# Moving the building of the diagonal tap weights in a two-layer decoder kernel

## The reference

```
def swiglu(x, w_gu, w_down):
    a, b = jnp.split(x @ w_gu, 2, axis=-1)
    return (jax.nn.silu(a) * b) @ w_down
...
for i in range(DEPTH):
    x = layer_norm(ALPHA * x + 0.5 * swiglu(x, ffn1_w_gu[i], ffn1_w_down[i]), ...)
    # layer 0: gated linear attention; layer 1: a causal depthwise convolution, 31 taps per channel
    ...
    x = layer_norm(ALPHA * x + concat([y, m]) @ w_out, ...)
    x = layer_norm(ALPHA * x + 0.5 * swiglu(x, ffn2_w_gu[i], ffn2_w_down[i]), ...)
```

## Time and profile before

| | us |
|---|---|
| three timed runs | 2041.99, 2045.09, 2046.26 |
| median | 2045.09 |
| span of the profiled execution | 2042.9 |
| TensorE busy | 2022.1 |
| VectorE busy | 1354.6 |
| ScalarE busy | 810.9 |
| GpSimd busy | 806.1 |

### The profile page before, as it was taken

One profiled execution on the slowest core, in us unless ns is written; L12 is line 12 of the kernel. 1 busy time (PEld: TensorE's weight loads), 2 busy tenths in 40 slices (PEclk: granted clock), 3 DMA queues, 4 the chain that ended last, 5 costly groups with the idle time before them and its releaser, 6 DMA issues.

```text
span 2042.9 us, 34356 instructions
## 1 busy us (share of the span) xinstructions
PE 2022.1 (99%) x13509; PEld 1855.9 (91%) x13509; DVE 1354.6 (66%) x1843; ACT 810.9 (40%) x1165; POOL 806.1 (39%) x513
## 2 busy tenths in 40 slices
PE   9999999999999999999999999999999999999998
PEld 9899998988988999999899999889887799999887
DVE  4477774553434768787456878646899886776645
ACT  5433352263423354444234444423453434434422
POOL 1588830033323348871015888001100435887000
PEclk9999999999999999999999999999999999999999
DMA  7533333332201234443232545233544322332232
GB/s 251 207 123 123 123 129 104 99 105 83 63 31 62 93 114 155 154 155 109 93 107 93 165 146 170 97 96 107 178 126 172 103 74 92 103 103 92 91 102 87
DMA packets 229514, 239.14 MB, mean 117 GB/s; under 512 B 5999, under 2 KB 222189, under 8 KB 227628
## 3 DMA queue, kind: packets, MB, share of 16 engines
q1 hardware_dynamic: 228780, 235.68, 35.3%
q10 hardware_dynamic: 640, 2.16, 0.3%
HBM read 215.80 MB, written 22.02 MB: 116 GB/s over the span
## 4 chain that ended last, share of the span: by engine, by line
PE 91%; POOL 3%; DVE 2%; ACT 2%; issue 1%; DMA 1%; DVEq 0%; SPq 0%; ACTq 0%; POOLq 0%
PE bank L1835 12%; PE bank L1837 12%; PE bank L1836 12%; PE bank L1964 11%; PE bank L1966 11%; PE bank L1965 11%; PE bank L1846 4%; PE bank L1847 4%; PE bank L1848 4%; PE bank L1918 1%; POOL wlo L532 1%; ACT whi L711 1%; PE bank L1923 1%; PE bank L2271 1%; PE bank L2270 1%
## 5 line engine op out<-in xcount | busy, mean ns | idle before, releaser
L711 ACT CAST whi<-raw 128x2048 fp32r<-128x2048 f32 (+3 forms) x190 | 322.1, 1696 | 868.0 <-POOL scratch L593 434.2
L1173 DVE TENSOR_TENSOR wlo<-raw,whi 128x2048 fp32r<-128x2048 f32 (+2 forms) x164 | 354.7, 2163 | 234.4 <-ACT whi L711 233.9
L570 POOL TENSOR_TENSOR tiny<-tiny 128x2 f32<-128x2 f32 (+1 forms) x13 | 9.4, 725 | 572.0 <-DVE tiny L1448 572.0
L589 POOL TENSOR_TENSOR raw<-raw 128x512 f32<-128x512 f32 x72 | 221.5, 3076 | 0.0
L1835 PE MATMUL bank<-h_hi,whi 128*128 128x512 f32 x528 | 207.1, 392 | 0.0
L1836 PE MATMUL bank<-h_lo,whi 128*128 128x512 f32 x528 | 205.5, 389 | 0.0
L1837 PE MATMUL bank<-h_hi,wlo 128*128 128x512 f32 x528 | 205.5, 389 | 0.0
L593 POOL TENSOR_TENSOR scratch<-raw,s 128x512 f32<-128x512 f32 x72 | 152.8, 2123 | 48.7 <-DVE ex_lo L1180 48.7
L1964 PE MATMUL bank<-t_hi,whi 128*128 128x256 f32 x576 | 163.7, 284 | 1.6 <-DVE bank L1240 1.6
L1964 PE MATMUL bank<-t_hi,ex_hi 128*128 128x256 f32 x576 | 163.7, 284 | 1.0 <-DVE bank L1232 0.5
L1965 PE MATMUL bank<-xlo,whi 128*128 128x256 f32 x576 | 163.0, 283 | 0.0
(11 more groups left out here) (363 smaller groups left out, 5938.2 us busy)
## 6 DMA issues: line engine op xcount, KB each, us to landing
raw<-in_ffn_w_gu_dram SPq DMA_DIRECT2D x88, 1024.0 KB, 4.9
raw<-in_ffn_w_down_dram SPq DMA_DIRECT2D x32, 896.0 KB, 5.0
raw<-in_ffn_w_down_dram SPq DMA_DIRECT2D x32, 512.0 KB, 3.4
raw<-in_gla_w_in_dram SPq DMA_DIRECT2D x14, 1024.0 KB, 5.1
early_raw<-in_conv_w_in_dram SPq DMA_DIRECT2D x18, 512.0 KB, 4.2
lo_scratch<-early_lo SPq DMA_DIRECT2D x18, 512.0 KB, 3.3
diag_scratch<-diag_tmp SPq DMA_DIRECT2D x8, 1024.0 KB, 7.6
raw<-in_conv_w_in_dram SPq DMA_DIRECT2D x16, 512.0 KB, 5.5
```

What stands on the lines that cost most here:

```text
L589: nc.gpsimd.tensor_tensor(a21, a21, a11, ALU.add).then_inc(w_sum, 1)
L711: nc.scalar.copy(whi[:, s, 0:kc, 0:width], raw[:, s, 0:kc, 0:width]).then_inc(hi_ready, 1)
L1173: nc.vector.tensor_tensor(wlo[:, s, 0:kc, 0:width], raw[:, s, 0:kc, 0:width], whi[:, s, 0:kc, 0:width].bitcast(F32), ALU.subtract).then_in ...
```

## The change

Batches 0 to 2 stay. Batches 3 and 4 are built after the last sums of the first block, where 6 and 7 stood, and no batch stands between the seven products. Batches 5, 6 and 7 are built by GpSimd in the second block after the norm that precedes it and ahead of its weight sums, and SyncE stores them between the loads of the second block's first chunks. A store now moves only the taps that a batch has (7 of 8 for batches 4 to 7). VectorE's wait in the first block is for five stores instead of eight, and SyncE waits for all eight before it loads early_raw in the second block.

```diff
--- before.py
+++ after.py
@@ -79,7 +79,7 @@
 GLU_EVAC = [2, 4, 6, 8, 14, 16, 18, 20]
 LATE = 3
 TAPS_K = [8, 8, 7, 7]
-DIAG_PAIR = [3, 5, 7]
+DIAG_DOWN = [3, 4]
 PE_TAPS = sum(TAPS_K)
 
 
@@ -347,7 +347,8 @@
 
                 def diagonal_store(d):
                     sp.wait_ge(diag_built, d + 1)
-                    sp.dma_start(diag_dram[d // 2, d % 2], diag_tmp[:, :, :].bitcast(F32)).then_inc(diag_stored, 16)
+                    kc = TAPS_K[d // 2]
+                    sp.dma_start(diag_dram[d // 2, d % 2, :, 0:kc, :], diag_tmp[:, 0:kc, :].bitcast(F32)).then_inc(diag_stored, 16)
 
                 if f == 0:
                     for i in range(FK // 2):
@@ -357,8 +358,6 @@
                         load(n0 + 2 * i + 1, 1, cols(w_gu, i * 256 + FF))
                         if i == 1:
                             diagonal_store(1)
-                        if i - 1 in DIAG_PAIR:
-                            diagonal_store(3 + DIAG_PAIR.index(i - 1))
                 else:
                     def gate_and_up(i):
                         load(n0 + 2 * i, 0, cols(w_gu, i * 256))
@@ -373,9 +372,20 @@
 
                     w_conv = a["conv_w_in"][0].rearrange("(k p) n -> p k n", p=P)
                     if f < 3:
+                        d = DIAG_DOWN[-1] + 1
                         gate_and_up(0)
-                        gate_and_up(1)
-                        gate_and_up(2)
+                        if f == 1:
+                            load(n0 + 2, 0, cols(w_gu, 256))
+                            diagonal_store(d)
+                            load(n0 + 3, 1, cols(w_gu, 256 + FF))
+                            diagonal_store(d + 1)
+                            load(n0 + 4, 0, cols(w_gu, 512))
+                            diagonal_store(d + 2)
+                            load(n0 + 5, 1, cols(w_gu, 512 + FF))
+                            sp.wait_ge(diag_stored, 16 * 2 * len(TAPS_K))
+                        else:
+                            gate_and_up(1)
+                            gate_and_up(2)
                         sp.wait_ge(x_ready, x_base((LN_GLA_OUT, LN_FFN[1])[f - 1]) + DK)
                         early_load(0)
                         with sp.Fori(3, FK // 2) as i:
@@ -398,10 +408,10 @@
                     sp.wait_ge(early_done, EARLY * f + 1)
                     early_store(EARLY - 1)
                 if f == 0:
-                    diagonal_store(6)
+                    diagonal_store(DIAG_DOWN[0])
                 down_loads(0, (2, 3))
                 if f == 0:
-                    diagonal_store(7)
+                    diagonal_store(DIAG_DOWN[1])
                 with sp.Fori(1, 4) as p:
                     down_loads(p, range(4))
 
@@ -627,9 +637,7 @@
             for i in range(PLAIN, FK // 2):
                 weight_sums(0, i, 0)
                 weight_sums(0, i, 1)
-                if i in DIAG_PAIR:
-                    diagonal(3 + DIAG_PAIR.index(i))
-            for d in (6, 7):
+            for d in DIAG_DOWN:
                 diagonal(d)
             norm(LN_FFN[0])
 
@@ -659,6 +667,8 @@
             spare_lo_parts(LN_GLA_OUT, GLA_OUT_N)
             split_lo_blocks(GLA_OUT_N + 7, 1, B_K, after_dve=True)
             norm(LN_GLA_OUT)
+            for d in range(DIAG_DOWN[-1] + 1, 2 * len(TAPS_K)):
+                diagonal(d)
             all_weight_sums(1)
             norm(LN_FFN[1])
             all_weight_sums(2)
@@ -1406,7 +1416,7 @@
                             for d in range(4, DK):
                                 scaled_x(ln, d)
                         if f == 0 and p == 0:
-                            dve.wait_ge(diag_stored, 16 * 2 * len(TAPS_K))
+                            dve.wait_ge(diag_stored, 16 * (DIAG_DOWN[-1] + 1))
                         residual_pair(ln, p, n0 + 4 * p + 4, 0.5, DOWN_BANKS[p], (n0 + 4 * p + 5, 1, DOWN_K[1]),
                                       (4, 5) if p == 2 else ())
 
```

## The result

The changed kernel took 2052.02 us (median of 6 runs, 2050.26 to 2055.74) against 2044.63 us for the kernel before on the same chip (6 runs, 2041.77 to 2046.26): ratio 1.0035, 95% interval 1.0026 to 1.0045. It is slower by 0.35%, which is over the 0.2% that can be told from no change. The forecast was 2052.0. The profiled run is the shortest of the six, 2050.26 us, with a span of 2048.5 against 2042.9.

A forecast was written before the change was run, and what follows sets the result against it. TensorE, busy for 2022.1 of 2042.9 us, was taken as the bound. Terms -2.6 + 9.0 + 0.6 + 0.1 = +7.1 us on the median of 2045.09 gave 2052; 8-in-10 range 2043.5 to 2057.5.

The forecast's parts named there:

- The gain: First block: moving three builds and stores from between the products saves 2.6 us, bounds nothing and 3.79.
- The three waits: First block: TensorE's product waits for VectorE after builds between the products, starts 142.63, 176.62 and 225.28; these go.
- I take nothing: First block's down products: the now eight-tap build, 3.76 us for 3.33, adds at most 0.43 us, counted as nothing.
- the fourth wait: First block's last pair, at 286.90: TensorE's product waits 1.05 us for h_lo beside a build; it stays.
- The relay: Second block: one tile forces build, store, landing, build, store, landing, build, from 733.5 to 757.
- The rival in which the relay fits: Second block: landings under about 4.8 us let the builds fit; time 2042 to 2048, chance 0.23.
- The port: Second block: builds and VectorE's two-input instructions exclude each other; without this the sum would be some 2 us smaller.
- The late loads: Second block: loads queued behind stores wait for builds; fourth load goes at 738, ScalarE's cast moves from 739.89 to 746.
- The first sum: Second block: GpSimd's first weight sum starts at 757.9 instead of 749.06, 8.8 us late.
- Its slack: Second block: TensorE's second product has 1.06 us of slack behind the extra low parts, making the delay 7.8 us.
- the sums of the second chunk: Second block: they take the port twice instead of once before the extra parts; 1.3 us at most, 1.2 taken.
- The clock: Second block: TensorE's granted clock falls from 2.4 to 1.2 GHz after the waits; 0 to 1.5 us, 0.6 taken.

The follow-up runs named there:

- e1: Changed kernel with batches 5 to 7 neither built nor stored, stored batch 4 read instead: 2044.07 us, ratio 0.9997 to the kernel before.
- e4: Changed kernel, complete, with each store of the second block issued one load later: 2049.32 us, ratio 1.0019 to the kernel before.
- e8: Changed kernel with zero fills for the last three builds and each of their stores one load later: 2045.73 us, ratio 1.0006 to the kernel before.
- e3: Changed kernel with zero fills of the same length for the last three builds; stores, waits and queue kept: 2047.93 us, ratio 1.0017 to the kernel before.
- e5: Kernel before, complete, with batch 7 alone built later, after the fourth low part of the first block's down products: 2042.97 us, ratio 0.9987.
- e2: Changed kernel with batches 5 to 7 built back to back, not stored, loads in the old order: 2049.51 us, ratio 1.0029 to the kernel before.
- e6: Complete; batch 3 after pair 3, 4 after the last sums, 5 to 7 in three blocks' down products: 2041.36 us, ratio 0.9987 to the kernel before.
- e7: Complete; only batch 7 built in the second block, 5 and 6 in the first block's down products: 2048.96 us, ratio 1.0025 to the kernel before.
- e9: e7 with its one second-block store issued one load later: 2046.31 us, ratio 1.0002 to the kernel before.

## Why the prediction was right, step by step

The time, 2052.02 against 2052.0, is nearer than the steps are.

**The gain, forecast 2.6.** Six profiles have this first block (the changed kernel, e1 to e4 and e8). Their matmuls are 2.1 to 2.7 us ahead at the end of the products and 1.9 to 2.7 ahead after the last pair; in the changed kernel it is 2.49 and 1.92. The three waits went as said. "I take nothing" for the eight-tap build in the down products doesn't always hold, since the fourth wait grew in four of the six (1.46, 1.3, 1.4 and 1.1 us; 0.9 in e3 and e8):

```profile
284.99 0.39 PE L1974 MATMUL bank<-t_hi,whi 128*128 128x256 f32 x1 [1.46 <-DVE bank L1250]
```

1.46 us idle against 0.89 in the earlier trace rows. The weight split ahead of it on VectorE, beside the build, took 2.31 us at 279.58; before, the same one took 1.74, and 1.22 in e5 without a build beside it. The build began 0.46 us ahead of the split, where before it was 1.03; the eight-tap build in front of it is 0.43 us longer. e5 shows this wait to be the build's, since it goes with it.

**The relay, forecast 23.5 us long, ending 757.** Measured 4.32 + 5.03 + 3.84 + 4.84 + 4.54 = 22.6 us. The builds cost more than the 3.9 taken and the landings less than the 5.6. The rival in which the relay fits needed landings of less than about 4.8 us with builds of 3.4. e8 comes to that, with landings of 4.04 and 4.82 and a relay of 18.9 us: it cost 3.2 us in the second block, where the first block had gained 2.7, and its time can't be told from that of the kernel before. So the relay by itself doesn't make the kernel slower; it takes the builds' reads, or the late loads, on top.

**The port, an addition of "some 2 us".** The sizes were right. The prediction let the x sums beside the first build end the third chunk's split 2.6 us late (738.38 to 741); it was 2.7 (4.87 us behind the norm's end before, 7.55 after). It gave t_lo 3 us beside the third build (755 to 758), and it was 2.99. It gave each build about a microsecond, and the three took 0.99, 0.51 and 1.21 more. (The "1.4 us more" that it read for the h_lo pair is 1.5, 2.77 against 1.29 in e5.) What it had wrong is the weight: "without it the sum below would be some 2 us smaller". Without the reads (e3) the cost is 3.8 us smaller, and with the builds alone (e2), no store and no late load, it is 7.3. The relay was put first, and by itself it cost less than half of what the builds did. In the changed kernel the three ends tie, which hid this from the forecast of the time.

**The late loads.** Forecast: fourth load at 738, cast at 746 instead of 739.89, 6.1 later. The cast came 743.22 - 731.38 = 11.84 us after the norm's end, 6.38 before: 5.5 later. That "all three releases come at about the same time" is what was measured, relay at 753.91 and t_lo at 754.99, the first sum at 755.33. The raw weights came earlier than the 755 forecast: the second late load landed at 744.93 + 7.08 = 752.01.

**The first sum, forecast 8.8 us late:** 24.0 - 15.6 = 8.4. **Its slack, 1.06, and the sums of the second chunk, 1.2 at most:** from the first sum to the end of the extra low parts it is 768.88 - 755.33 = 13.55 us against 12.75, so 0.8. That gives 8.4 - 1.06 + 0.8 = 8.1, and TensorE's second product started at 768.93, 8.2 us late: 6.06 later than in the earlier trace rows, where the norm's end came 2.13 later.

**The clock, forecast 0.6:** from the second product on the matmuls fell another 1.6 us behind (6.06 to 7.65). The fall was twice as long as those of the kernel before, and what of it lay outside the waits was underrated. The cost of the block comes out at 9.6 to 9.8 where 9.7 was said: the first sum and the second chunk 0.8 too dear, the clock and the pairs behind 0.9 too cheap. That these cancel is luck.

**The rest of the kernel, forecast nothing:** -2.0 us in this profile (7.65 behind to 5.66). 1.5 of it is a clock fall near 1650 us that this execution doesn't have, 1.2 are waits of before that it doesn't have later in the second block, and 0.7 is lost in the third. No step of the change is there, and e1, without the three batches, differs from the kernel before in the same way at 1650 and in the third block, so I take it for chance; the other five runs are 0.5 to 5.5 us longer. On the medians the change is 7.4 us, against 7.1 in the sum.

The waits of TensorE were forecast as "some 5 us" before the first product and "2 to 3" before the second. They were 3.9 and 1.4, and a third of 1.4 came before the third chunk, of which the prediction spoke as contained. The matmuls were 0.21 us apart behind them, as written. One sum of the prediction is off: its low case, 3.8 - 1.06 - 2.6, is +0.1 and not "about +1", so 2045 and not 2046; nothing rests on it.

## What to carry to other kernels

An engine's idle time is free for a piece of work only if what the piece shares is idle too. Here GpSimd had 15.5 us with nothing to do, but VectorE was at work nearly all of that time and its two-input instructions and GpSimd's builds kept each other waiting; one build at the same price, put where both were idle (e5, e6), cost nothing. Look for places where two columns of the timeline are empty, not one.

When several late things release one instruction, test each alone and not only by taking it away: removing the loads' delay from the whole brought 1 us of 9.6, while one late load behind a single build had cost 3 (e7 against e9).

## What the runs showed of the hardware that I had not expected

The clock falls come and go between runs of nearly the same work. Before, the profile has three ahead of its last 8 us (windows, columns as above):

```profile
445.97:449.37 3.40, 3.40 (x8) 0.50 0.94 296
626.88:630.28 3.40, 3.40 (x9) 0.50 0.02 5
1647.46:1650.86 3.40, 3.40 (x18) 0.50 0.66 218
```

In the changed kernel those near 445 and 625 are there and the one near 1650 isn't, though the wait of 2.0 us ahead of it is:

```profile
1652.00:1656.00 4.00, 1.97 (x16) 1.00 0.05 12
```

In e6 the two near 625 and 1650 are missing (its first, near 444, is there):

```profile
618.00:630.00 12.00, 12.00 (x68) 1.00 0.00 1
1639.00:1652.00 13.00, 10.96 (x91) 1.00 0.25 82
```

Each is worth 1.5 to 1.6 us by the starts of the matmuls, of which a wait behind it can give some back. Over the 29 runs of the kernel before in the second comparison the time and TensorE's mean granted clock go together (correlation -0.77, in the other two -0.81 with 26 runs and -0.89 with 19); one kernel spreads over 2040 to 2049 us, and the falls are probably a good part of that, though only the profiled executions show where they stood. What decides whether a given wait is followed by a fall stays open. Of the 6.35 us by which e6's profile is ahead at its end, 3.1 come at the two missing falls, and 0.6 of them are lost again by 700 us; only the 2.9 of the first block stand where the edit acts.

A load behind a store on SyncE's queue: alone a 1 MB load landed 4.90 to 4.95 us after its issue (three loads of e9), right behind a store of 896 KB it took 7.06 to 7.08 us in the changed kernel. The three stores took 4.93, 4.75 and 4.24 us there. In e4 the first two, with no load issued behind them at once, took 3.49 and 3.59; but its third took 4.78 and e8's third 5.40, with no load behind them either, so the load isn't all that lengthens a store, and what else does stays open.
